# Key columns projected inside the first normalization, and keys prepared inside the projection

## The reference, cut to what matters

```python
h = layer_norm(concatenate([meta, x]), ln0_g, ln0_b)        # 2064 tokens x 1024
proj = h @ w_in                                             # 4040 columns
qa, ka, va, qb, cb, qi, ki, wi, gates = split(proj, ...)
y_a = swa_sink_attention(qa, ka, va, sinks) @ w_o_a         # window of 128 keys + meta tokens
c_kv = rms_norm(cb, kv_norm_g)                              # latent keys, 128 wide
k_idx = layer_norm(ki, k_idx_g, k_idx_b)                    # indexer keys, 64 wide
y_b = dsa_mla_attention(qb, c_kv, qi, k_idx, wi, ...) @ w_o_b   # top 256 keys of the indexer
g = sigmoid(gates + b_gate)
h = layer_norm(ALPHA * h + (g_a * y_a + g_b * y_b) @ w_out, ...)
h = layer_norm(ALPHA * h + SwiGLU(h), ...)
```

## Time and profile before

| | us |
|---|---|
| median of 3 runs | 4401.1 (4399.94 to 4422.27) |
| the profiled execution | 4415.0 |
| its span, first to last instruction | 4413.2 |

### The profile page before, as it was taken

One profiled execution on the slowest core, in us unless ns is written; L12 is line 12 of the kernel. 1 busy time (PEld: TensorE's weight loads), 2 busy tenths in 40 slices (PEclk: granted clock), 3 DMA queues, 4 the chain that ended last, 5 costly groups with the idle time before them and its releaser, 6 DMA issues. The chain is left out here.

```text
span 4413.2 us, 55060 instructions
## 1 busy us (share of the span) xinstructions
PE 3822.9 (87%) x18481; PEld 3151.3 (71%) x18481; DVE 1517.5 (34%) x2420; ACT 1685.5 (38%) x2759; POOL 1656.6 (38%) x2005
## 2 busy tenths in 40 slices
PE   2899999736888888888996899988999799988998
PEld 2788888614666677777885688866887588866886
DVE  8000000045567788888541411043101411033111
ACT  1101122123566777777853234223432234222221
POOL 2111011024555555544312344543445344443443
PEclk9999999855688999999997899998999899998999
DMA  4212222120111010000002333342333333342332
GB/s 162 69 58 72 72 71 68 61 57 17 32 28 27 18 26 24 20 13 13 14 16 79 119 91 95 115 153 72 99 115 105 124 90 95 115 157 69 98 95 86
DMA packets 368453, 321.14 MB, mean 73 GB/s; under 512 B 18120, under 2 KB 327528, under 8 KB 364168
## 3 DMA queue, kind: packets, MB, share of 16 engines
q1 hardware_dynamic: 361296, 300.88, 22.6%
q10 hardware_dynamic: 6976, 17.90, 1.1%
HBM read 258.79 MB, written 59.94 MB: 72 GB/s over the span
## 5 line engine op out<-in xcount | busy, mean ns | idle before, releaser
L1600 POOL TENSOR_TENSOR ff_w_lo<-ff_raw,ff_w_hi 128x1024 fp32r<-128x1024 f32 x328 | 794.9, 2424 | 1018.5 <-ACT ff_w_hi L1647 1018.5
L96 PE MATMUL ff_bank<-ff_h_hi,ff_w_lo 128*128 128x512 f32 x1664 | 660.9, 397 | 99.9 <-POOL ff_w_lo L1600 83.3
L97 PE MATMUL ff_bank<-ff_h_hi,ff_w_hi 128*128 128x512 f32 x1664 | 656.8, 395 | 0.0
L98 PE MATMUL ff_bank<-ff_h_lo,ff_w_hi 128*128 128x512 f32 x1664 | 656.0, 394 | 0.0
L1647 ACT ACTIVATE ff_w_hi<-ff_raw 128x1024 fp32r<-128x1024 f32 x328 | 345.9, 1055 | 761.4 <-PE ff_bank L98 757.0
L96 PEld LDWEIGHTS ff_bank<-ff_h_hi,ff_w_lo 128*128 128x128 f32 x1664 | 318.4, 191 | 176.7 <-issue 110.7
L96 PE MATMUL in_acc<-pj_h_hi,in_w_lo 128*128 128x512 f32 x1024 | 407.1, 398 | 11.6 <-POOL in_w_lo L316 11.6
L1010 PE MATMUL at_ctx<-at_p_t,keys_c_nat 128*128 128x128 f32 (+1 forms) x2432 | 375.1, 295 | 43.6 <-ACT at_ctx_t L1167 43.1
L97 PE MATMUL in_acc<-pj_h_hi,in_w_hi 128*128 128x512 f32 x1024 | 407.8, 398 | 0.0
L98 PE MATMUL in_acc<-pj_h_lo,in_w_hi 128*128 128x512 f32 x1024 | 407.8, 398 | 0.0
L1010 PEld LDWEIGHTS at_ctx<-at_p_t,keys_c_nat 128*128 128x128 f32 (+1 forms) x2432 | 321.2, 200 | 87.3 <-ACT at_ctx_t L1167 63.7
(11 more groups left out here) (235 smaller groups left out, 6121.1 us busy)
## 6 DMA issues: line engine op xcount, KB each, us to landing
ff_raw<-in_w_ff_gate SPq DMA_DIRECT2D x88, 512.0 KB, 3.8
ff_raw<-in_w_ff_up SPq DMA_DIRECT2D x88, 512.0 KB, 3.8
ff_raw<-in_w_ff_down SPq DMA_DIRECT2D x88, 512.0 KB, 3.3
proj<-in_row SPq DMA_DIRECT2D x28, 1024.0 KB, 4.7
in_raw<-in_w_in SPq DMA_DIRECT2D x32, 512.0 KB, 5.9
ff_gates<-proj SPq DMA_DIRECT2D x64, 256.0 KB, 2.8
ff_raw<-in_w_out SPq DMA_DIRECT2D x32, 512.0 KB, 3.4
ln_x<-in_x SPq DMA_DIRECT2D x16, 512.0 KB, 3.4
```

Source lines behind the costliest of these rows:

```text
L96: pe.matmul(out, lhs_lo, rhs_hi, start=start, stop=False)
L97: pe.matmul(out, lhs_hi, rhs_hi, start=False, stop=False)
L98: return pe.matmul(out, lhs_hi, rhs_lo, start=False, stop=stop)
L1600: pool.tensor_tensor(w_lo[u][:, :], raw[u][:, :], f32(w_hi[u][:, :]), ALU.subtract).then_inc(lo_ready[u], 1)
```

## The change: what it does

`prepare_keys` is gone as a stage; its work is done inside `project`, which now has two blocks.

*First block, normalization with the key chunks.* The token tiles go in the order 8 tiles, meta tokens, 8 tiles. The tile's work is divided anew: VectorE takes statistics and centers, ScalarE multiplies by the inverse root (`scale`), GpSimd adds the shift (`add_shift`), in three buffers for the normalized tile. The weights of the four key chunks are loaded, and their high parts (ScalarE, `hold`) and low parts (GpSimd) are held in the SBUF space that the keys will take. Behind the transposes of a tile TensorE computes one group (24 matmuls) of one key chunk, when the 512 tokens of the group are there: 12 such sums behind tiles, then the four of the last group and four short ones for the meta tokens. ScalarE copies each sum, SP stores it. SP, no longer ScalarE, stores the normalized tiles. The weights of the first two other chunks are loaded at the end of the block.

*Second block, the other 28 chunks with the key tiles.* In each of the first 17 chunks one key tile is prepared: its three transposes stand ahead of the chunk's matmuls (for tile 0 behind the first group), its two transposes back behind the third group. One buffer each instead of two. Each group of a chunk has its own row buffer and its own store of 256 KB. The stores to `v_nat` go through SP. All loops are written out.

```diff
 first block
+            TOKENS = [(META + P * i, P, P * i) for i in range(8)] + [(0, META, None)] + [(META + P * i, P, P * i) for i in range(8, SEQ // P)]
+            SUMS = [(g, c) for g in range(NG) for c in range(len(KEY_CHUNKS))] + [(NG, c) for c in range(len(KEY_CHUNKS))]
...
+                    load(0)
                     sp.dma_start(gain[:, :], ...)
+                    load(1)
                     sp.dma_start(shift[:, :], ...)
+                    for c in range(2):
+                        sp.dma_start(raw[c][:, :, :], columns(KEY_CHUNKS[c])).then_inc(w_loaded[c], 16)
...
+                    for i in range(NT):                       # SP
+                        if i + 2 < NT:
+                            load(i + 2)
+                        if 0 <= i - 2 < 2:
+                            sp.wait_ge(held_lo_ready, i - 1 + START)
+                            sp.dma_start(raw[i % 2][:, :, :], columns(KEY_CHUNKS[i])).then_inc(w_loaded[i % 2], 16)
+                        store(i)
+                        if i:
+                            for _ in sums_behind(i - 1):
+                                store_sum(done)
...
+                    for i in range(NT):                       # GpSimd
+                        inverse_root(i)
+                        if i:
+                            add_shift(i - 1)
+                        if i < len(KEY_CHUNKS):
+                            pool.wait_ge(held_hi_ready, i + 1 + START)
+                            pool.tensor_tensor(held_lo[i], raw[i % 2][:, :, :], f32(held_hi[i]), ALU.subtract).then_inc(held_lo_ready, 1)
...
+                    for i in range(NT):                       # VectorE
+                        statistics(i)
+                        if i >= 2:
+                            low_part(i - 2)
...
+                    for i in range(NT):                       # TensorE
+                        turn(i)
+                        for _ in sums_behind(i):
+                            sums(done)
...
+                    for i in range(NT):                       # ScalarE
+                        scale(i)
+                        if i < len(KEY_CHUNKS):
+                            hold(i)
+                        if i:
+                            high_part(i - 1)
+                        if i >= 2:
+                            for _ in sums_behind(i - 2):
+                                copy_sum(done)
 second block
+                    for n in range(NC):                       # SP
+                        if n + 2 < NC:
+                            load_weights(n + 2)
+                        load_bias(n)
+                        if n < NK:
+                            sp.wait_ge(square_ready, n + 1 + START)
+                            sp.dma_start(v_nat[...], vn[0:rows, :]).then_inc(v_stored, 16)
+                            if n + 1 < NK:
+                                load_keys(n + 1)
+                        for g in range(NG):
+                            sp.wait_ge(acc_copied[g], n + 1 + START)
+                            sp.dma_start(proj[...], row[g][:, :]).then_inc(stored[g], 16)
...
+                    for n in range(NC):                       # GpSimd: low_part(n + 1), then root and copy of key tile n
...
+                    for n in range(NC):                       # TensorE
+                        u = n % 2
+                        if 0 < n <= NK - 1:
+                            turn_keys(n)
+                        pe.wait_ge(lo_ready, n + 1 + START)
+                        for g in range(NG):
+                            if n:
+                                pe.wait_ge(acc_copied[g], n + START)
+                            ...  24 matmuls into acc[g]
+                            if n == 0 and g == 0:
+                                turn_keys(0)
+                            if g == 2 and n < NK:
+                                turn_back(n)
...
+                    for n in range(NC):                       # ScalarE
+                        if n + 1 < NC:
+                            high_part(n + 1)
+                        if n < NK:
+                            squares(n)
+                        if gate:
+                            evacuate(n, 0)
+                        evacuate(n, 1)
+                        if gate:
+                            evacuate(n, 2)
+                        if n < NK:
+                            high_keys(n)
+                        evacuate(n, 3)
...
+                        if n < NK:                            # VectorE
+                            normalize(n)
+                        if n and not gate:
+                            evacuate(n, 0)
+                        if not gate:
+                            evacuate(n, 2)
+                        if n < NK:
+                            low_keys(n)
```

More of the change, by code:

```diff
@@ L228, in _, with turn @@
-                    tiles(pe, turn)
+                    def turn(i):
+                        n = TOKENS[i][1]
+                        pe.wait_ge(h_ready, i + 1 + START)
+                        if i >= 2:
+                            pe.wait_ge(lo_ready, i - 1 + START)
+                        for c in range(KT):
+                            last = pe.transpose(turned[i % 2][:, c, 0:n], hb[i % 3][0:n, c * P:c * P + P], ident[0:n, 0:n])
+                        last.then_inc(turned_ready, 1)
@@ L259, in project, with gates_before @@
+            (w_loaded, hi_ready, lo_ready, bias_loaded, acc_ready, acc_copied, stored, g_loaded, key_loaded, nat_ready, square_ready, var_ready,
+             rstd_ready, norm_ready, copied, back_ready, key_hi, key_lo, v_stored) = later
+            NC = len(OTHERS)
+            KEY_TILES = [(j, min(P, L - j)) for j in range(0, L, P)]
+            NK = len(KEY_TILES)
+            def gates_before(n):
+                return sum(OTHERS[m] >= SPLIT_CHUNKS for m in range(n % 2, n, 2))
             with nc.Block() as block:
@@ new lines, in _ @@
+                    low_part(0)
+                    for n in range(NC):
+                        if n + 1 < NC:
+                            low_part(n + 1)
+                        if n < NK:
+                            first, rows = KEY_TILES[n]
+                            pool.wait_ge(var_ready, n + 1 + START)
+                            pool.tensor_tensor(rstd[0:rows, :], var_eps[0:rows, :], half[0:rows, :], ALU.pow).then_inc(rstd_ready, 1)
+                            pool.wait_ge(norm_ready, n + 1 + START)
+                            pool.tensor_copy(c_nat[0:rows, first:first + P], cn[0:rows, :]).then_inc(copied, 1)
@@ new lines, in low_keys, with evacuate @@
+                    def low_keys(j):
+                        first, n = KEY_TILES[j]
+                        dve.wait_ge(key_hi, j + 1 + START)
+                        dve.tensor_tensor(c_lo[:, first:first + n], back[:, 0:n], f32(c_hi[:, first:first + n]), ALU.subtract)
+                        dve.tensor_tensor(ki_lo[:, first:first + n], back[:, P:P + n], f32(ki_hi[:, first:first + n]), ALU.subtract).then_inc(key_lo, 1)
+                    def evacuate(n, g):
+                        dve.wait_ge(acc_ready[g], n + 1 + START)
+                        if n:
+                            dve.wait_ge(stored[g], 16 * n + START)
+                        dve.tensor_copy(row[g][:, :], acc[g][:, :]).then_inc(acc_copied[g], 1)
```

585 lines of the change are left out of this document (265 added, 320 removed).

## The result

The changed kernel takes 4295.7 us (median of 4 runs, 4287.8 to 4302.6); the kernel before took 4404.1 beside it. The ratio is 0.9743, with an interval of 0.972 to 0.9765; the two medians alone give 0.9754, inside it. Measured again, against other runs of before, it was 0.9735 (0.9718 to 0.9753). The forecast of 4280 was 15.7 us low. The profiled executions compare more closely: the kernel before took 4415.0, the changed kernel 4302.6, and the forecast by the profile was 4293.5. So the miss to be explained is 9.1 us.

What follows compares the result with a forecast made beforehand. Projection bound by TensorE's matmuls, key stage by a relay; the gain is when attention can start. +66 first stage, -93.5 projection, -93.3 key stage, -0.7 gap: -121.5, so 4280 us from the median (4293.5 by profile); range 4250 to 4335.

Steps and rivals of the forecast that it cites:

- start-up, to the fifth turn: First block until the fifth tile's transposes: 59 us, set by GpSimd's order and late weight loads; bounds 45 and 75.
- 13 slots and the last group's sums: First block's steady state: 13 tile slots at 6.6 plus 2.3, 88 us; then four sums of 5.57, 22 us.
- four meta sums: End of first block: four groups of 24 16-column matmuls for the meta tokens, 2.6 us each, 10 us.
- hand-over to the projection: Between the blocks: last sum's copy and store, barrier, then the weight's high and low parts, 8 to 9 us.
- projection with 17 key tiles: Second block: 28 chunks at 22.4 us, 627, plus 13 for the key tiles' transposes, 640 instead of 733.5.
- end gap: Between projection and attention: 4.5 us instead of 5.2, as the last store is 256 KB instead of 1 MB.
- from attention's start to the end: From attention's first GpSimd operation: the same 3459 us; clock effect costed at nothing, 20 us either way as bounds.
- the key stage: Separate key preparation between projection and attention, a relay with no engine half busy: its removal saves 93.3 us.
- bounds of +50 and +98: First stage: limits on the projection's later start, forecast at +66 us (188 instead of 122.2).
- Rival C: Projection and first stage: transposes drop the clock, 1.6 us per insertion, 73 us more, total 4353; chance 0.08.
- two loops: First block's steady state: two dependency loops compete with TensorE; one has slack, the other is level, 13.1 against 13.0 us.
- second loop: First block: sum copy, SP's store, then token load, statistics, root and shift; 13.1 us for two tiles.

Runs made afterwards that it cites:

- meta_pairs: Changed kernel with the meta tokens' 16-column matmuls alternated, three by three, with the last group's 512-column ones; 4276.7 us from one execution, projection starting at 188.2.
- keys_only: Kernel before with only the key tiles moved into the projection, five chunks late, normalization as before; 4331.7 us, ratio 0.9827.
- sums_only: Changed kernel with key preparation put back as its own stage behind a 28-chunk projection; 4371.5 us, ratio 0.992 against the kernel before.
- early_weights: Changed kernel with the last two held key-chunk weights loaded in the second pass of SyncE's loop; projection starts at 183.5 us, span 4277.5, one execution.
- load_first: Changed kernel with SyncE loading token tiles ahead of its waits for partial sums; projection starts at 189.5 us, span 4284.5, one execution.
- Changed_again: The changed kernel run once more with nothing edited; 4291.2 us (4288.6 to 4302.0).

## Why the prediction was right, and where its sizes were off

| term | predicted | measured |
|---|---|---|
| start-up, to the fifth turn | 59 | 59.8 |
| 13 slots and the last group's sums | 88 + 22 | 110.6 (59.8 to 170.4) |
| four meta sums | 10 | 17.5 |
| hand-over to the projection | 8 to 9 | 5.8 (187.9 to 193.7) |
| projection with 17 key tiles | 640 | 639.9 |
| end gap | 4.5 | 3.4 |
| from attention's start to the end | 3459 | 3463.7 |

The mechanism was right in its main parts: what the key stage and the key tiles cost and bring, what sets the start-up, and that the two halves add. Taken from the profiled time, the miss of 9.1 us is the first stage, +5.7 (+7.1 for the meta sums, since 4 x 2.6 is 10.4; +1.1 before them; -2.7 for the hand-over; 0.2 of rounding); the gap, -1.1; and +4.7 behind attention's start; these make 9.3, and the 0.2 is rounding. The bounds of +50 and +98 were added up wrongly: their own terms (45 + 85 + 32 + 8, and 75 + 112 + 32 + 9, less 122) make +48 and +106. The measured +71.5 lies in either.

**The term that was mis-sized is "four meta sums 4 x 2.6".** The prediction took 2.6 us from the earlier trace rows, where a single meta group stands between 512-column matmuls, and saw there that the clock falls only *behind* the 24 short ones. Four such groups in a row were priced as four single ones. In the row of four the fall comes at the same place, at 173.3, 0.3 us behind the copy of the first; and here three more short groups stand where the earlier trace rows has 512-column matmuls, and pay 4.7, 5.1 and 5.1 us instead of 2.6. meta_pairs shows it: alternated, the price is the predicted one. Rival C had the clock falling, but behind the transposes of key tiles; that didn't happen: 17 tiles cost 11 us (keys_only) and 14 us (sums_only against changed) where it needs 54 in the projection.

**The hand-over** was overpriced by 2.7 us. The last sum to be stored is a meta sum, 8 KB that land in 1.4 us, and not the 256 KB that the prediction priced at 3: ScalarE's high part began 2.25 us after the last copy, and 3.5 us later the matmuls.

**The start-up** came out for the reason given: GpSimd waited 7.67 and 7.9 us for the third and fourth held chunk, and early_weights took 10.7 us off it by moving the loads alone. The shifts were forecast to end at 22, 28, 42, 55.5 and 59, and the turns behind them began at 24.8, 30.1, 42.9, 56.0 and 59.8. The first two are late, among other things by the 2.2 us of semaphore updates and a table load of 1.28 us on ScalarE (15.07), which no term holds. The two rounds of a held chunk behind them were priced at 14 and 13.5 us and took 12.8 and 13.1, which takes most of that back: so near a hit is partly luck. As to the meetings of engines that were weighed there, VectorE's centering took 2.50 instead of 1.28 us where it met GpSimd's shift, and GpSimd's root took 0.55 us where it ran apart from VectorE's large passes, 1.33 to 1.64 beside them. The Trainium skill (SBUF — State Buffer, § SBUF: two separate sides) calls the port pair of these two engines an exclusive lock that the first one holds for its whole instruction. The trace agrees: in the steady state the root starts 0.13 us into a centering of 1.28, takes 1.56 and ends 0.4 us behind it. What these meetings cost in all was not measured by itself.

**The steady state** was level only in the worst place. The prediction's two loops, "level" at 13.1 against 13.0 us, gave slots of 6.6; TensorE set 6.48 everywhere but at the meta tile, which has no sum behind it. There the relay shows: 5.2 us of wait and 2 us at the lower clock. The wait is mostly the second loop's, as load_first shows (1.9 us are left without it), so that loop was rightly drawn but not level everywhere. The sum, 110 against 110.6, came so near because two errors cancel, 0.12 us too much in each of twelve slots and the 2 us at the lower clock behind the meta tile, which no term has. That is luck too.

**The other half of the gain** stands as predicted: the two halves alone gave -79.3 and -38.3 us at the start of attention, together -117.6; the whole change gave -117.2 (954.2 to 837.0). So they hardly touch each other: the four key chunks cost the projection less, and the tiles find the same cover in either.

**Attention.** Its unchanged stretch (first turn to the feed-forward stage) took 1339 to 1362 us over the thirteen executions of the table, and the feed-forward stage 2000 to 2003. Changed_again, the same kernel, differs by 10 us from its first execution. From attention's first GpSimd instruction to the end it took 3452.7 us, 6.3 less than the kernel before. So the 4.7 us are within what repeats differ by, and no cost of the change is shown. The stretch was longest (1361.6) with the lowest clock in its first 342 us (0.70) and shortest (1339.3) with the highest (0.78); between them the order isn't strict. What sets that clock from run to run stays open. The 15.7 us between the forecast and the median are the 9.1 and a difference between profile and median: the profiled execution lay 14 us above the median before and 7 above it after.

## What to carry to other kernels

Price a row of short matmuls by a row of them, not by one group between long ones; if the clock falls inside it, alternate them with long ones instead of putting them at the end. Before a chain is divided over more engines, ask whether the engine that it leaves is late at all: here a lone VectorE at 5.46 us a tile was ahead of TensorE's 6.48, and the division cost 21 us, in the start-up and at the one tile with no sum behind it, where TensorE had nothing else to do. Work that was moved into a neighbour whose TensorE is always busy cost here what TensorE itself does for it (0.65 to 0.82 us a key tile) and no more; its own waits, some 8 us by the prediction, were shorter than the 16.7 us of cover. And count the semaphores that a block sets up ahead of its first load.

## What the runs showed of the hardware

- TensorE falls to 1.2 GHz in back-to-back 16-column matmuls, with no wait between them: 0.11 us apart before 173.3, 0.21 after, at a granted clock of 0.50. With three 512-column matmuls to three short ones it stays at 1.00 to the last matmul (meta_pairs, 142 to 181.5).
- Three transposes, or two, between groups of 512-column matmuls do not make it fall: the matmul behind them takes 0.48 us, the next 0.39.
- GpSimd's two-input pass held VectorE's centering until it ended (2.50 us instead of 1.28), but not VectorE's low part with one input in PSUM (1.21 to 1.23 us in 14 meetings). GpSimd's 128-value root took 0.55 us apart from VectorE's large passes and 1.33 to 1.64 beside them.
- A semaphore update on SyncE takes 0.06 us: 58 of them put the first load at 4.16 us, 43 at 3.28 (sums_only), 20 at 1.93.
- The same kernel differs by 10 us in one unchanged stretch between two executions, while the 940 us ahead of it repeat within 0.8.
